# Attention with a running bound: rough tiles with a causal mask are computed inside exact tiles with a mask, the others in rounds without masks, four in every round

## The chip, the cores and the metric

The kernel runs on one core of one Trainium2 chip. Its engines are named as in the profile: PE is TensorE's matmul, PEld its weight load, DVE is VectorE, ACT is ScalarE, POOL is GpSimd, SP is SyncE, which here issues most of the DMAs. The metric is the time of one execution on the device, in microseconds (us). Three runs of the kernel before took 3304.9, 3312.74 and 3315.3 us; the median, 3312.74 us, is what the change is compared with.

## The reference, cut to what matters

A decoder of two layers over a sequence of 2048 tokens and 1024 channels: a gated DeltaNet layer, then a cross-decoder layer with "forgetting attention". Only the attention is touched. It has 16 heads of width 64; for query t and key s, with F the cumulated log forget gates:

```python
for blk in range(seq // B_BLOCK):
    ...
    logits = (jnp.einsum('bhqd,bhkd->bhqk', q[:, :, s0:s1], k[:, :, :s1]).astype(jnp.float32)
              + log_f_cum[:, :, s0:s1, None] - log_f_cum[:, :, None, :s1])
    causal = jnp.arange(s0, s1)[:, None] >= jnp.arange(s1)[None, :]
    p = jax.nn.softmax(jnp.where(causal, logits, -jnp.inf), axis=-1)
    outs.append(jnp.einsum('bhqk,bhkd->bhqd', p.astype(v.dtype), v[:, :, :s1]))
...
return (o * jax.nn.silu(z)) @ w_out
```

The softmax needs, for every query, something near the largest logit to subtract before the exponential.

## The kernel before

**The stages.** The program is five stages one after the other: projection and solve of the DeltaNet layer, its recurrence, an output projection, then `projections_and_attention` (the tiles whose names begin with `at_`), then a second output projection. Only `projections_and_attention` is changed. It first makes K, Q, V and the gate z of all heads by matmuls of a 128x128 weight with 512 columns, in 8 groups of 16 tiles of 24 matmuls each, and stores them to memory. Then comes the attention.

**Units and rounds.** A unit is a pair of heads p (0 to 7) and a block of 512 queries qb (0 to 3): 32 units, numbered u, for pair 0 with qb = 0, 1, 2, 3 and for every other pair with qb = 3, 2, 1, 0. Unit u covers 4(qb+1) key tiles of 128 keys; a round R handles two of these key tiles for both heads, so a unit has 2(qb+1) rounds and there are 160 rounds. From round 20 on the pattern repeats every 20 rounds (one pair of heads): 8, 6, 4 and 2 rounds.

**Exact tiles.** In a round PE makes four exact tiles of logits (keys on the partitions, queries along the free axis): a first pass over 67 rows (L1904) and a second over 128 rows (L1907), both in the format f32r and both up to 512 columns wide. In the last two rounds of a unit the key tiles cross the diagonal: the tiles are 512, 384, 256 or 128 columns wide, and a bf16 matmul of the identity with `mask_k` (L1906) adds the causal mask to 128 columns, between the two passes. ACT takes each tile through Exp (L2298); PE then multiplies the exponentials of the round before with V (L1922: eight matmuls for two key tiles), and DVE (head 0, L2146 and L2138) and POOL (head 1, L1685 and L1680) add up the exponentials for the denominator. At a unit's end, one round later, PE sums these over the partitions (L1936).

**Rough tiles.** The value that is subtracted is a row maximum of rough logits, found before the unit begins: for each head and each of four groups of 128 queries (`sub`), a one-pass matmul over 66 rows (L1890) against each block of 512 keys (`grp`), in a bank of PSUM out of three, which DVE reduces to its maximum (L2083). Where `grp == qb` the tile crosses the diagonal: it is (sub+1)*128 columns wide and gets the mask by a bf16 matmul with `mask_q` (L1893). I call these masked rough tiles and the others, always 512 wide, whole ones. There are 640 rough tiles: 384 whole and 256 masked. A rough tile on PE waits until DVE has reduced the one three places earlier (`reduced.wait(pe, j - 3)`).

**The order of the rough tiles** is a table made by Python code: `ITEMS` lists them unit by unit with `grp` innermost, and `ROUGHS[slot]` says which of them are done in which slot. The last 8 tiles of the projections (slots -8 to -1) are each followed by 6 rough tiles; after that the code spreads the rest over the rounds so that each unit is ready four rounds before it starts, which comes to 4 in most rounds, and 3 or 2 after round 132. In a round, each exact tile is followed by one rough tile. When the last rough tile of a unit is reduced, at the end of round `TURN[u]` PE transposes the maxima (L1944), ACT copies them (L2240) and issues two DMAs (L2243) that put them as a row into the tile of queries; the unit's first exact tile waits for them (`top_in`).

**The loads.** SP loads the keys, queries, gates and values of pair p+2 into the buffers of pair p, block by block of 512 positions: for each block `load_one` (the rows that the rough tiles need, L1704), `load_gates` (L1707), `load_two` (L1715), `load_values` (L1721), 2 MB in all. For p of 1 and more each block is loaded when the unit that used it last is done; for pair 0 all four blocks of pair 2 (first 3, then 2, 1, 0) are loaded one after the other when unit 3 is done, in round 21. The first rough tile of a unit waits for all blocks it needs.

## Time and profile before

| | |
|---|---|
| median of three runs (lowest, highest) | 3312.74 us (3304.9, 3315.3) |
| profiled execution: time, span | 3323.32 us, 3321.7 us |
| mean granted clock of TensorE in it | 0.962 of full speed |
| PE, DVE, ACT, POOL busy in the span | 3072.7, 1749.2, 1241.4, 1062.4 us |
| rough tiles: PE matmuls without masks (L1890), DVE reductions (L2083) | 238.0 us, 372.5 us (640 of each) |
| exact tiles: first pass, second pass, Exp on ACT | 263.3 us, 256.0 us, 332.1 us (640 of each) |

The profiled execution lasted 10.6 us longer than the median of the three others, within their spread on the high side. A duration of a PE matmul in the trace includes the way through the array: successive matmuls of 512 columns overlap, so what counts for the sum is the distance from one start to the next. The engine to look at is PE, and the stretch is the attention: from 2259.56 us (first rough tile) to about 3111 us of the span.

### The profile page before, as it was taken

How to read it: one execution, taken by the hardware profiler on the slowest of the kernel's cores; microseconds unless marked ns; L12 is line 12 of the kernel's file. 1: busy time of each engine (PE TensorE's matmuls, PEld its weight loads, DVE VectorE, ACT ScalarE, POOL GpSimd, SP SyncE). 2: the span in 40 equal slices, each digit the busy share in tenths (PEclk: the TensorE clock that was granted, in tenths of full speed). 3: DMA queues.
4: the chain of work that ended last, by engine and by line, in shares of the span. 5: the costliest groups of instructions: out<-in, count | busy, mean ns of one | idle time of the engine just before them, and what ended most of it. 6: DMA issues, size and time to landing. Idle time of an engine off the chain costs nothing. (4 is left out here: it accounts for less than half of the span.)

```text
span 3321.7 us, 40715 instructions
## 1 busy us (share of the span) xinstructions
PE 3072.7 (93%) x15148; PEld 2310.0 (70%) x15148; DVE 1749.2 (53%) x2715; ACT 1241.4 (37%) x2163; POOL 1062.4 (32%) x765
## 2 busy tenths in 40 slices
PE   5999899999987997995899999999999999999799
PEld 3766667888767886784687888887555555555487
DVE  4555564567464665554322221113777777777433
ACT  4245445554413554324322211210444444445411
POOL 0488970223216552110000000000355445555310
PEclk8999999999998999997899999998899999999899
DMA  5233431576736664556443431216353433330343
GB/s 217 65 132 109 136 107 52 180 231 185 236 99 211 209 201 151 184 179 186 114 114 107 125 102 70 76 60 143 90 128 96 115 85 88 87 90 10 108 152 120
DMA packets 259823, 427.86 MB, mean 129 GB/s; under 512 B 74126, under 2 KB 154646, under 8 KB 254508
## 3 DMA queue, kind: packets, MB, share of 16 engines
q1 hardware_dynamic: 220572, 323.54, 33.0%
q0 software_dynamic: 22960, 86.08, 8.3%
q10 hardware_dynamic: 16112, 15.86, 1.5%
q8 instruction: 111, 1.82, 0.2%
q14 instruction: 68, 0.56, 0.1%
HBM read 274.58 MB, written 150.69 MB: 128 GB/s over the span
## 5 line engine op out<-in xcount | busy, mean ns | idle before, releaser
L2298 ACT ACTIVATE at_probs<-at_ps 128x512 f32<-128x512 f32 (+3 forms) x640 | 332.1, 534 | 363.5 <-PE at_ps L1907 299.5
L2083 DVE TENSOR_REDUCE at_partial<-at_ps 128x1 f32<-128x512 f32 (+3 forms) x640 | 372.5, 606 | 161.1 <-PE at_ps L1890 121.7
L106 PE MATMUL pa_y<-pa_h_high,pa_w_high 128*128 128x512 f32 x1056 | 422.0, 400 | 12.8 <-ACT pa_acc L772 7.1
L108 PE MATMUL pa_y<-pa_h_high,pa_w_low 128*128 128x512 f32 x1056 | 412.7, 391 | 0.0
L107 PE MATMUL pa_y<-pa_h_low,pa_w_high 128*128 128x512 f32 x1056 | 412.5, 391 | 0.0
L1685 POOL TENSOR_TENSOR at_plain<-at_plain,at_probs 128x512 f32<-128x512 f32 (+3 forms) x256 | 308.2, 1204 | 230.1 <-ACT at_probs L2298 215.0
L1825 PE MATMUL at_ps<-at_h_high,at_w_high 128*128 128x512 f32 x768 | 301.2, 392 | 30.0 <-DVE at_w_low L2013 28.2
L1826 PE MATMUL at_ps<-at_h_low,at_w_high 128*128 128x512 f32 x768 | 300.2, 391 | 0.0
L1827 PE MATMUL at_ps<-at_h_high,at_w_low 128*128 128x512 f32 x768 | 300.1, 391 | 0.0
L1904 PE MATMUL at_ps<-at_h_low,at_h_high 67*128 67x512 f32 (+3 forms) x640 | 263.3, 411 | 10.8 <-ACT at_probs L2298 10.6
L1907 PE MATMUL at_ps<-at_h_low,at_h_high 128*128 128x512 f32 (+3 forms) x640 | 256.0, 400 | 0.0
L1890 PE MATMUL at_ps<-at_h_high,at_h_low 66*128 66x512 f32 (+3 forms) x640 | 238.0, 377 | 7.7 <-DVE at_partial L2083 6.6
L106 PEld LDWEIGHTS pa_y<-pa_h_high,pa_w_high 128*128 128x128 f32 x1056 | 199.3, 189 | 64.4 <-issue 15.7
L2146 DVE TENSOR_TENSOR at_plain<-at_plain,at_probs 128x512 f32<-128x512 f32 (+3 forms) x256 | 220.6, 862 | 19.1 <-ACT at_probs L2298 18.3
L107 PEld LDWEIGHTS pa_y<-pa_h_low,pa_w_high 128*128 128x128 f32 x1056 | 199.4, 189 | 43.8 <-issue 3.6
L108 PEld LDWEIGHTS pa_y<-pa_h_high,pa_w_low 128*128 128x128 f32 x1056 | 199.0, 188 | 42.3
L1904 PEld LDWEIGHTS at_ps<-at_h_low,at_h_high 67*128 67x128 f32 x640 | 124.3, 194 | 115.2 <-issue 81.8
L570 DVE SCALAR_TENSOR_TENSOR pa_acc<-pa_ybuf,pa_taps,pa_acc 128x2048 f32<-128x2048 f32 x72 | 196.7, 2733 | 2.6
L1825 PEld LDWEIGHTS at_ps<-at_h_high,at_w_high 128*128 128x128 f32 x768 | 145.2, 189 | 60.3 <-issue 28.6
L407 POOL TENSOR_SCALAR pa_gb<-pa_gb,pa_csil 128x1024 f32<-128x1024 f32 x48 | 169.6, 3534 | 30.3 <-DMA pa_gb<-in_a_mod_w_dram 20.7
L1827 PEld LDWEIGHTS at_ps<-at_h_high,at_w_low 128*128 128x128 f32 x768 | 145.0, 189 | 30.6
L1826 PEld LDWEIGHTS at_ps<-at_h_low,at_w_high 128*128 128x128 f32 x768 | 145.1, 189 | 30.0
(350 smaller groups left out, 5560.1 us busy)
## 6 DMA issues: line engine op xcount, KB each, us to landing
at_h_low<-s_Q SPq DMA_DIRECT2D x96, 256.0 KB, 7.1
s_qkv<-pa_sil POOLq DMA_DIRECT2D x16, 1024.0 KB, 6.6
pa_sil<-s_qkv SPq DMA_DIRECT2D x16, 1024.0 KB, 6.6
dr_kv<-s_qkv SPq DMA_DIRECT2D x16, 1024.0 KB, 8.7
s_K<-at_parts SPq DMA_DIRECT2D x64, 256.0 KB, 4.2
s_Q<-at_parts SPq DMA_DIRECT2D x64, 256.0 KB, 4.1
at_h_high<-s_K SPq DMA_DIRECT2D x32, 512.0 KB, 5.6
pa_wraw<-in_a_w_in_dram ACTq DMA_DIRECT2D x15, 1024.0 KB, 6.1
```

Source lines behind the costliest of these rows:

```text
L106: nc.tensor.matmul(out, w_high[:, k], h_high[:, k], start=k == 0, stop=False)
L107: nc.tensor.matmul(out, w_high[:, k], h_low[:, k], start=False, stop=False)
L108: ins = nc.tensor.matmul(out, w_low[:, k], h_high[:, k], start=False, stop=k == KC - 1)
L1685: g_summed.done(g_.tensor_tensor(to[:, off:BLK], to[:, off:BLK], xs[:, t, off:BLK], ALU.add))
L1825: mm(Y[b % NB], w_high[:, k, at], h_high[:, n, k], start=k == 0, stop=False)
L1826: mm(Y[b % NB], w_high[:, k, at], h_low[:, n, k], start=False, stop=False)
L1827: ins = mm(Y[b % NB], w_low[:, k, at], h_high[:, n, k], start=False, stop=k == KC - 1)
L1890: ins = mm(bank[:, 0:width], Q1[p % 2][0:DH + 2, h, q_at], K1[p % 2][0:DH + 2, h, grp * BLK:grp * BLK + width], start=True, stop=grp < qb)
L1904: mm(out, K1[s][0:DH + 3, h, k_at], Q1[s][0:DH + 3, h, q_at], start=True, stop=False)
L1907: logits_ok.done(mm(out, K2[s][:, h, k_at], Q2[s][:, h, q_at], start=False, stop=True))
L2083: reduced.done(v.tensor_reduce(partial[:, u % 2, h * NQ + sub, grp:grp + 1], rough[:, j % 3, 0:width], AX.X, ALU.max))
L2298: probs_ok.done(a.activation(probs[:, R % 2, t, h, off:BLK], logits[:, l % 3, off:BLK], ACT.Exp))
```

## The change

The list of rough tiles is no longer in the order of units. `whole(u)` gives the whole tiles of unit u, by falling `grp` and with heads and `sub` inside; `masked(u)` its eight masked ones. The eight slots behind the last projection tiles take 8 rough tiles each in place of 6: masked tiles of unit 0, whole and masked ones of unit 1, and the whole ones of units 2 and 3. In the rounds, the last two rounds of every unit (those whose exact tiles have a mask) take four masked rough tiles; the other rounds after round 6 take four whole ones; a round for which the list is empty takes none. That is so in rounds 2, 3, 6, 143 to 145, 148 to 151 and 154 to 159.

On PE the place of a rough tile inside its round changes too. In a round with masks, the rough matmul is issued between the exact tile's first pass and its mask, and the two mask matmuls stand one behind the other. In a round without masks nothing changes: a rough tile still follows each exact tile. A rough tile now waits for the two blocks it reads (`grp` and `qb`) instead of the unit's first one waiting for all. The partial maxima get room for eight units instead of two (`partial`).

Units are ready (`TURN`) in other rounds than before; rounds 48 to 67 stand for the repeating pattern:

| unit (pair, qb) | starts in round | maxima turned, before | after |
|---|---|---|---|
| 10 (2, 1) | 54 | 46 | 48 |
| 11 (2, 0) | 58 | 48 | 54 |
| 12 (3, 3) | 60 | 56 | 58 |
| 13 (3, 2) | 68 | 62 | 61 |

The diff, whole but for the context:

```diff
-    ITEMS = [(u, h, sub, grp) for u, (_, qb) in enumerate(UNITS) for h in range(2) for sub in range(NQ) for grp in range(qb + 1)]
-    ITEM_END = [2 * NQ * sum(qb + 1 for _, qb in UNITS[:u + 1]) for u in range(len(UNITS))]
+    def whole(u):
+        return [(u, h, sub, grp) for grp in reversed(range(UNITS[u][1])) for h in range(2) for sub in range(NQ)]
+
+    def masked(u):
+        return [(u, h, sub, UNITS[u][1]) for h in range(2) for sub in range(NQ)]
 
     EARLY = 8
-    PER_TILE = ITEM_END[2] // EARLY
+    ITEMS = masked(0) + whole(1) + masked(1) + whole(2) + whole(3)
+    PER_TILE = len(ITEMS) // EARLY
     ROUGHS = {s - EARLY: range(s * PER_TILE, (s + 1) * PER_TILE) for s in range(EARLY)}
-    DONE = ITEM_END[2]
+    wholes = [x for u in range(NB, len(UNITS)) for x in whole(u)]
+    maskeds = [x for u in range(2, len(UNITS)) for x in masked(u)]
     for R in range(ROUNDS):
-        due = [(ITEM_END[u] - DONE, max(START[u] - 4, 0)) for u in range(len(UNITS)) if ITEM_END[u] > DONE]
-        take = max([-(-n // (d - R + 1)) for n, d in due if d >= R], default=0)
-        ROUGHS[R] = range(DONE, DONE + take)
-        DONE += take
-    TURN = {u: 1 + next(s for s in ROUGHS if ITEM_END[u] - 1 in ROUGHS[s]) for u in range(len(UNITS))}
+        of = maskeds if R >= START[UNIT_OF[R] + 1] - 2 else wholes if R > START[2] else []
+        ROUGHS[R] = range(len(ITEMS), len(ITEMS) + min(4, len(of)))
+        ITEMS += of[:4]
+        del of[:4]
+    UNIT_END = [max(j for j, x in enumerate(ITEMS) if x[0] == u) for u in range(len(UNITS))]
+    UNIT_BEGIN = [min(j for j, x in enumerate(ITEMS) if x[0] == u) for u in range(len(UNITS))]
+    TURN = {u: 1 + next(s for s in ROUGHS if UNIT_END[u] in ROUGHS[s]) for u in range(len(UNITS))}
...
-                if j == 0 or ITEMS[j - 1][0] != u:
-                    for n in range(qb + 1):
+                if h == 0 and sub == 0:
+                    for n in (grp, qb):
                         pe.wait_ge(one_in[p % 2][n], (p // 2 + 1) * ONE)
...
-                if grp == qb:
-                    ins = mm(bank[:, sub * P:width], ident_b[:, :], mask_q[:, :], start=False, stop=True)
-                rough_ok.done(ins)
-
-            def exact_logits(R, t, kb, off, h):
+                if grp < qb:
+                    rough_ok.done(ins)
+
+            def mask_rough(j):
+                u, h, sub, grp = ITEMS[j]
+                if grp == UNITS[u][1]:
+                    rough_ok.done(mm(rough[:, j % 3, sub * P:(sub + 1) * P], ident_b[:, :], mask_q[:, :], start=False, stop=True))
+
+            def exact_logits(R, t, kb, off, h, beside):
...
                 if kb >= qb * NQ:
+                    for j in beside:
+                        rough_logits(j)
                     mm(logits[:, l % 3, off:off + P], ident_b[:, :], mask_k[:, :], start=False, stop=False)
+                    for j in beside:
+                        mask_rough(j)
                 logits_ok.done(mm(out, K2[s][:, h, k_at], Q2[s][:, h, q_at], start=False, stop=True))
+                if kb < qb * NQ:
+                    for j in beside:
+                        rough_logits(j)
...
-                            exact_logits(R, t, kb, off, h)
-                            for j in items[(2 * t + h) * part:(2 * t + h + 1) * part]:
-                                rough_logits(j)
+                            exact_logits(R, t, kb, off, h, items[2 * t + h:2 * t + h + 1])
```

Two places show what PE is given. The first is PE at the start of round 66, the first masked round of unit 12 (`at_h_low,at_h_high` is an exact pass, `at_h_high,at_h_low` a rough tile, `at_mask_k` and `at_mask_q` the masks). Before:

```order
L1904 MATMUL at_ps<-at_h_low,at_h_high 128x512
L1906 MATMUL at_ps<-at_mask_k,at_ident_b 128x128
L1907 MATMUL at_ps<-at_h_low,at_h_high 128x512
L1890 MATMUL at_ps<-at_h_high,at_h_low 128x128
L1893 MATMUL at_ps<-at_mask_q,at_ident_b 128x128
L1904 MATMUL at_ps<-at_h_low,at_h_high 128x512
L1906 MATMUL at_ps<-at_mask_k,at_ident_b 128x128
L1907 MATMUL at_ps<-at_h_low,at_h_high 128x512
```

The same place in the changed program, where L1915 and L1922 are the exact passes, L1897 the rough tile, L1919 and L1905 the masks:

```order
L1915 MATMUL at_ps<-at_h_low,at_h_high 128x512
L1897 MATMUL at_ps<-at_h_high,at_h_low 128x128
L1919 MATMUL at_ps<-at_mask_k,at_ident_b 128x128
L1905 MATMUL at_ps<-at_mask_q,at_ident_b 128x128
L1922 MATMUL at_ps<-at_h_low,at_h_high 128x512
L1915 MATMUL at_ps<-at_h_low,at_h_high 128x512
L1897 MATMUL at_ps<-at_h_high,at_h_low 128x256
L1919 MATMUL at_ps<-at_mask_k,at_ident_b 128x128
```

The rough matmul moved ahead of the exact tile's mask, and the two bf16 matmuls are neighbours. The second place is PE in slot -7, behind the second of the last eight projection tiles. Before, six rough tiles and the first matmul of the next projection tile:

```order
L1890 MATMUL at_ps<-at_h_high,at_h_low 128x384
L1893 MATMUL at_ps<-at_mask_q,at_ident_b 128x128
L1890 MATMUL at_ps<-at_h_high,at_h_low 128x512
L1893 MATMUL at_ps<-at_mask_q,at_ident_b 128x128
L1890 MATMUL at_ps<-at_h_high,at_h_low 128x512
L1890 MATMUL at_ps<-at_h_high,at_h_low 128x128
L1893 MATMUL at_ps<-at_mask_q,at_ident_b 128x128
L1890 MATMUL at_ps<-at_h_high,at_h_low 128x512
L1890 MATMUL at_ps<-at_h_high,at_h_low 128x256
L1893 MATMUL at_ps<-at_mask_q,at_ident_b 128x128
L1838 MATMUL at_ps<-at_w_high,at_h_high 128x512
```

In the changed program the same slot has eight whole rough tiles in a row (one row with its count), and then the first transpose of maxima and the next projection tile:

```order
L1846 MATMUL at_ps<-at_w_low,at_h_high 128x512
L1847 MATMUL at_ps<-at_w_high,at_h_low 128x512
L1897 MATMUL at_ps<-at_h_high,at_h_low 128x512 x8
L1962 MATMUL at_ps<-at_ident,at_top 8x128
L1845 MATMUL at_ps<-at_w_high,at_h_high 128x512
```

Six of the eight slots look like this one; slots -8 and -6 have eight masked rough tiles.

## Rows read from the trace of the kernel before

**Rows 1.** Stretches: us, busy PE, PEld, DVE, ACT, POOL (instructions), PEclk, DMA share, GB/s.

```profile
2259.56:2330.95 71.39, 64.94 (x243) 47.87 (x242) 28.39 (x56) 0.53 (x2) 6.96 (x2) 0.86 0.59 140
2330.95:2360.22 29.27, 29.27 (x91) 17.21 (x90) 17.50 (x28) 9.66 (x19) 7.71 (x8) 0.53 0.95 220
2360.22:2437.51 77.29, 76.64 (x374) 42.91 (x372) 65.25 (x98) 36.79 (x70) 40.37 (x33) 1.00 0.03 11
2437.51:2536.85 99.34, 96.79 (x486) 54.22 (x484) 75.69 (x125) 47.62 (x92) 48.98 (x41) 1.00 0.63 141
2536.85:3025.54 488.69, 480.68 (x2413) 270.09 (x2411) 375.21 (x618) 237.96 (x460) 250.26 (x206) 1.00 0.35 88
3025.54:3106.13 80.59, 79.73 (x390) 41.65 (x388) 58.77 (x78) 41.90 (x81) 46.50 (x37) 1.00 0.04 14
```

**Rows 2.** Waits in rounds 48 to 67: engine, line, releaser, us, times, longest.

```profile
PEld at_ps L1904 <- ACT at_probs L2298: 2.8, 4, 0.8
```

**Rows 3.** Timeline of a burst of six rough tiles, slot -5: start, us, instruction.

```profile
2288.06 0.69 DVE L2074 TENSOR_TENSOR at_parts<-at_ps,at_row 128x512 f32<-128x512 f32 x1 [6.35 <-PE at_ps L1840]
...
2288.67 3.27 DVE L2083 TENSOR_REDUCE at_partial<-at_ps 128x1 f32<-128x512 f32 x6
...
2290.71 0.57 PE L1838 MATMUL at_ps<-at_w_high,at_h_high 128*128 128x512 f32 x1
```

**Rows 4.** The same columns for rounds 51, 54, 55, 66 and 67.

```profile
2591.82:2596.76 4.94, 4.94 (x24) 2.78 (x22) 4.69 (x7) 2.40 (x4) 2.87 (x3) 1.00 0.06 22
...
2605.87:2609.70 3.83, 3.83 (x24) 2.78 (x22) 2.77 (x5) 2.39 (x4) 0.20 (x1) 1.00 0.00 0
2609.70:2615.49 5.79, 5.79 (x27) 3.06 (x25) 5.74 (x9) 3.62 (x6) 4.69 (x4) 1.00 0.52 133
...
2664.99:2670.27 5.28, 5.28 (x31) 2.70 (x30) 3.89 (x9) 2.18 (x4) 2.88 (x3) 1.00 0.00 0
2670.27:2675.17 4.90, 4.43 (x32) 2.68 (x30) 2.67 (x7) 1.37 (x5) 1.41 (x3) 1.00 0.02 4
```

**Rows 5.** Timeline of masks in rounds 66 and 67, PE.

```profile
2668.22 0.23 PE L1893 MATMUL at_ps<-at_mask_q,at_ident_b 128*128 128x128 bf16 x1
2668.38 0.65 PE L1922 MATMUL at_ps<-at_probs,at_parts 128*64 128x512 f32 x2
...
2670.48 0.23 PE L1906 MATMUL at_ps<-at_mask_k,at_ident_b 128*128 128x128 bf16 x1
...
2670.72 0.23 PE L1890 MATMUL at_ps<-at_h_high,at_h_low 66*128 66x128 f32 x1
```

**Rows 6.** Timeline: PE, fourth exact tile of round 67, behind the transpose for unit 14.

```profile
2672.72 0.33 PE L1904 MATMUL at_ps<-at_h_low,at_h_high 67*128 67x128 f32 x1 [0.47 <-ACT at_probs L2298]
```

**Rows 7.** Timeline, SP: last DMA issued for block 3 and for block 2 of pair 2.

```profile
2447.71 1.48 SPq L1721 DMA_DIRECT2D at_wraw<-s_ZT  x1
...
2453.34 0.51 SPq L1721 DMA_DIRECT2D at_wraw<-s_ZT  x1
```

**Rows 8.** The same loads: DMA issues from 2447.6 and from 2453.2 us, us to landing.

```profile
at_wraw<-s_ZT SPq DMA_DIRECT2D x1, 256.0 KB, 9.2
at_wraw<-s_ZT SPq DMA_DIRECT2D x1, 256.0 KB, 13.3
```

**Rows 9.** Timeline, PE: first rough tile of round 23, and of round 28.

```profile
2452.65 0.40 PE L1890 MATMUL at_ps<-at_h_high,at_h_low 66*128 66x512 f32 x1
2452.88 0.40 PE L1904 MATMUL at_ps<-at_h_low,at_h_high 67*128 67x512 f32 x1
...
2479.19 0.51 PE L1890 MATMUL at_ps<-at_h_high,at_h_low 66*128 66x512 f32 x1 [0.53 <-DMA at_h_high<-s_Fp]
```

**Rows 10.** The clock around an idle PE of the first stage, and in rounds 0 to 3.

```profile
347.40:352.10 4.70, 0.00 (x0) 0.00 (x0) 0.00 (x0) 4.64 (x3) 4.62 (x3) 1.00 0.44 121
352.20:355.50 3.30, 2.89 (x4) 1.34 (x5) 0.00 (x0) 3.28 (x6) 3.30 (x2) 0.50 0.95 308
...
2332.00:2359.20 27.20, 27.20 (x82) 16.40 (x82) 16.45 (x26) 9.57 (x19) 6.69 (x7) 0.50 0.98 229
```

More of the change, by code:

```diff
@@ L1537, in projections_and_attention @@
         mask_q, mask_k = st.sb("mask_q", [P, P], BF16), st.sb("mask_k", [P, P], BF16)
-        partial = st.sb("partial", [P, 2, 2 * NQ, NB])
+        partial = st.sb("partial", [P, 2 * NB, 2 * NQ, NB])
         top = st.sb("top", [P, 2, 2 * NQ])
@@ L1960, in _ @@
                                 rough_logits(j)
+                                mask_rough(j)
                             for u in turned_in(slot):
@@ L1979, in _ @@
                         pe.wait_ge(top_in, 32 * (u + 1))
-                    part = -(-len(items) // 4)
                     for t, kb, off in tiles(R):
                         for h in range(2):
-                            exact_logits(R, t, kb, off, h)
-                            for j in items[(2 * t + h) * part:(2 * t + h + 1) * part]:
-                                rough_logits(j)
+                            exact_logits(R, t, kb, off, h, items[2 * t + h:2 * t + h + 1])
                 for summed in ended(R, 1):
@@ L2079, in reduce @@
                 width = BLK if grp < qb else (sub + 1) * P
-                if j == 0 or ITEMS[j - 1][0] != u:
-                    top_ok.wait(dve, u - 2)
+                if j == UNIT_BEGIN[u]:
+                    top_ok.wait(dve, u - 2 * NB)
                 rough_ok.wait(dve, j)
-                reduced.done(v.tensor_reduce(partial[:, u % 2, h * NQ + sub, grp:grp + 1], rough[:, j % 3, 0:width], AX.X, ALU.max))
-                if j == ITEM_END[u] - 1:
+                reduced.done(v.tensor_reduce(partial[:, u % (2 * NB), h * NQ + sub, grp:grp + 1], rough[:, j % 3, 0:width], AX.X, ALU.max))
+                if j == UNIT_END[u]:
                     reduced.wait(dve, j)
                     turned_ok.wait(dve, u - 2)
-                    top_ok.done(v.tensor_reduce(top[:, u % 2], partial[:, u % 2, :, 0:qb + 1], AX.X, ALU.max))
+                    top_ok.done(v.tensor_reduce(top[:, u % 2], partial[:, u % (2 * NB), :, 0:qb + 1], AX.X, ALU.max))
             make_columns(0)
```

## The prediction

> **What bounds the kernel now.** I read the stretches of the attention first [rows 1]. In all of them PE is busy for 91 to 100% of the time, DVE for 40 to 84%, ACT and POOL for less: PE bounds the attention. Beside the first two stretches the granted clock is 1.00. The waits come next: in rounds 48 to 67, 98 us long, PE's largest wait for another engine is 2.8 us in four times [rows 2]. So a change pays here only if it shortens PE's own sequence, and costs wherever PE is made to stand still. Then I read the one place where PE already waits for DVE, the bursts of rough tiles between projection tiles [rows 3], single rounds [rows 4], single masks [rows 5], what follows the transpose of the maxima [rows 6], the loads that rough tiles wait for [rows 7 to 9], and the clock after an idle PE [rows 10]. All sums are for the profiled execution (3323.32 us, its span 3321.7); the median of the three runs is 3312.74, 10.6 us lower, and I add the difference to that.
>
> **The bursts, +8.8 us.** PE runs at most three rough tiles ahead of DVE. In a burst DVE first takes the projection tile (its start is 0.26 us into the burst), then starts its reductions 0.61 us later, and six of them took 3.27 us, which is 0.6 us from one 512-column start to the next (the narrow ones less) [rows 3]. The burst of six ended 2.92 us after its start of 2287.79 (at 2290.71). With eight whole tiles the last one waits for the fifth reduction: 0.88 us to the first, four more starts of 0.6, 0.73 from a start until PE goes on, and 0.23 for the tile itself: 4.24 us. With eight masked tiles the fifth reduction starts at 0.88 + 1.6 = 2.5 us, and the burst is 3.1 us long. So 6 x 4.24 + 2 x 3.1 = 31.6 us. Before, the eight bursts took 2.3 to 3.2 us each in the timeline, 22.8 us of the stretch of 71.39 us; the other 48.6 us are seven projection tiles at a clock of 0.86 on the mean [rows 1]. I take these as unchanged: the clock falls after the bursts already now, and can hardly fall more often than once in each.
>
> **Rounds 0 to 3, -4.3 us.** They took 29.27 us at a mean clock of 0.53 [rows 1]. Sixteen rough tiles become eight narrow ones; in rounds 2 and 3 eight tiles go without anything in their place. At half clock a 512-column pass is 0.43 us: eight are 3.4 us, and the narrower tiles of rounds 0 and 1 make 0.9.
>
> **The rounds with and without masks.** A full round with four whole rough tiles: round 51 took 4.94 us with one masked tile of full width [rows 4], and a mask before the values costs 0.16 us from L1893 to L1922 [rows 5], against 0.10 where the values follow a f32r pass: 4.87. A unit's first round, whose values are those of narrow tiles: 3.83 less the mask, more 128 columns, 3.82. With the sums of the unit before: 5.79 - 0.07 = 5.72. Round 66, four masked rough tiles already, becomes 5.28 - 0.25 = 5.03; round 67, 4.90 with a stall of 0.66 [rows 6], becomes 4.11; unit 11's two rounds, with the same reckoning, 3.95 and 4.97.
>
> The stalls behind `turn_top`: ACT copies the maxima and issues two DMAs ahead of its next Exp, and an exact tile of the next round waits for it, with an engine idle for 0.47 us in round 67 [rows 6] (0.66 more than usual from start to start) and 0.45 in a full round. After the change three of four fall in full rounds, one in a short one that is at that tile 0.1 us sooner: 3 x 0.45 + 0.76 = 2.1 us.
>
> Twenty rounds are then 6 x 4.87 + 3 x 5.72 + 3 x 3.82 + 3 x 5.03 + 3.95 + 3 x 4.11 + 4.97 + 2.1 = 96.3 us, against 98.2 in the trace, -1.9. Rounds 40 to 139: 5 x 96.3 = 481.5 against 488.69, -7.2 (the last seven rounds had three rough tiles before). Rounds 4 to 19 in the same way: 75.7 against 77.29, -1.6. Rounds 140 to 157, where eleven rounds lose their rough tiles and four take masked pairs: 77.6 against 80.59, -3.0; POOL's and DVE's work there (46.5 and 58.8 us [rows 1]) stays covered.
>
> The Trainium skill ("TensorE: Matmul & The Clock Gate", Architectural detail) says that PE pulls weight loads ahead of matmuls in flight. By that a lone mask would cost its columns alone and the pairing nothing: the sum would come out some 8 us later. The 0.24 us above speak against it.
>
> **A new wait, +6.4 us less 0.9.** Rough tiles of unit 8 move from round 28 to round 23, and the first needs block 2 of pair 2. In the trace these blocks arrive in order under a saturated DMA: the last DMA of block 3 was issued at 2447.71 [rows 7] and landed 9.2 us later [rows 8], at 2456.9; that of block 2, issued at 2453.34, landed at 2466.6. What the rough tile waits for is the first quarter of block 2's bytes: 2456.9 + 9.7/4 = 2459.3. The cross-check is round 28, where the first rough tile waited for block 0 until 2479.19 [rows 9], two blocks or 20 us later. PE would be at that rough tile at 2452.65 [rows 9], plus 0.25 for rounds 21 and 22 as changed: 2452.9. It stands there 6.4 us, and behind it in PE's queue are three exact tiles of round 23, for which ACT, DVE and POOL wait. The 0.9 us of round 28 go. Nothing else can hide this, since all work of PE is in that queue. Block 1, needed in round 25, comes in time. Rounds 20 to 39: 96.3 + 6.4 = 102.7 against 99.34, +3.4 (the 0.9 is in the 99.34).
>
> **The clock behind it, +6 us.** An idle PE of 4.7 us in the first stage was followed by a clock of 0.50 [rows 10], the 1.2 GHz level, there for 3.4 us, until the clock was at 1.00 again while dense f32r passes of 128 rows ran. In the attention it took longer: from 2332.0 to 2359.2 the clock stayed at 0.50 with PE busy in all 27.2 us [rows 10], and rose inside the values of round 3, behind the sums of unit 0. So after the stall of round 23 I expect half clock. The bounds: 3.4 us of it, which costs 1.7; or until the sums in round 29, six rounds of about 4.2 us each, 25 us. Neither is nearer by its kind of work than the second, but the values at half clock last twice as long as now and may end it earlier; I take one and a half rounds, 6 us.
>
> The Trainium skill (same page, What's actually happening) has the gate open again after one busy window. By it the 6 would be 1.7. Rows 10 disagree for this stage, and the measurement decides.
>
> **Sum.** 8.8 - 4.3 - 1.6 + 3.4 - 7.2 - 3.0 + 6 = +2.1 us. 3312.74 + 2.1 = 3314.8; I say 3315.
>
> **Rivals.** (1) Slower by the clock: after round 23 it stays at 1.2 GHz until the sums of round 29, or does not come back in round 3: 3312.7 - 3.9 + 25 = 3334, and in between from 3323 on, when it lasts three rounds or more. For it: the 27.2 us [rows 10]. Against: the rise came with the values, and those run in each round. (2) DVE becomes the bound in rounds of four whole tiles. In round 51 it was busy for 4.69 of 4.94 us [rows 4]; a fourth whole tile in place of narrower ones adds up to 0.4 us in the others. If it lags 0.2 us in each of some 60 such rounds, +12: 3327. Against: DVE's lag may grow by three tiles, the two masked rounds of each unit give it time, and round 51 already is such a round and did not stall. (3) The second mask costs 0.13: 232 pairs x 0.07 = 16 us more, 3331; this is also the case that the pairing doesn't do what it says. (4) Faster: block 2 arrives in time, because its first DMAs pass the queue sooner than by their share of bytes. Then 6.4 and 6 go: 3302.5. For it: rough tiles wait for rows of only two blocks. Against: the order of landings above.
>
> **How the numbers follow.** My forecast 0.52; (1) 0.18, (2) 0.05, (3) 0.08, (4) 0.12, the skill's rule on weight loads 0.05 (3323). A run can be told from no change at about 0.3%, 10 us: under 3302.8 or over 3322.7. Slower: (1), (3), half of (2) and of the rule, 0.31. Faster: 0.10 of (4) and 0.06 for the forecast with a clock that rises at once and bursts cheaper than worked out, 0.16. The rest, 0.53, is no difference. Range: 3301 to 3331; my forecast alone 3306 to 3322.
>
> **What would show it.** Bursts of 4.2 us between projection tiles; in masked rounds 0.18 us for both masks; rounds 51 and 66 at 4.87 and 5.03; 96.3 us for rounds 48 to 67; a wait of some 6 us of PE in round 23 for a DMA into `at_h_high`, and a PEclk of 0.5 behind it. A stretch of 98 us for rounds 48 to 67 would refute the pairing, no wait in round 23 the fifth term, and a clock of 1.00 behind that wait the sixth.

## The result: 0.43% slower, and the profile after

The changed kernel took 3328.07 us (median of 6 runs, 3322.8 to 3331.8), the kernel before 3314.02 us beside it (6 runs, 3304.9 to 3332.5): a ratio of 1.0043 with a 95% interval of 1.0023 to 1.0064. The 14 us more lie in the predicted range (3301 to 3331), but above the 3306 to 3322 of the forecast alone, and on the side that had a chance of 0.31, not on the likeliest one, "no difference".

The profiled execution of the changed kernel took 3328.63 us. Its stretches, in the columns of [rows 1]: us, busy PE, PEld, DVE, ACT, POOL, PEclk, DMA share, GB/s:

```profile
2264.57:2342.02 77.45, 69.88 (x252) 48.33 (x250) 39.98 (x73) 0.53 (x2) 6.96 (x2) 0.90 0.55 134
2342.02:2363.58 21.56, 20.54 (x87) 12.19 (x85) 9.67 (x19) 9.12 (x19) 6.68 (x7) 0.72 1.06 236
2363.58:2439.78 76.20, 75.47 (x377) 42.14 (x375) 57.94 (x94) 36.41 (x70) 40.11 (x34) 1.00 0.07 25
2439.78:2547.21 107.43, 98.97 (x486) 55.70 (x485) 79.41 (x125) 47.45 (x92) 46.70 (x41) 0.95 0.59 133
2547.21:3031.55 484.34, 476.17 (x2423) 270.85 (x2421) 393.96 (x625) 237.25 (x460) 241.16 (x206) 1.00 0.35 89
3031.55:3111.11 79.56, 77.03 (x374) 39.65 (x372) 43.83 (x67) 40.00 (x81) 45.33 (x37) 1.00 0.04 14
```

Line by line against [rows 1]: the last projection tiles with their bursts +6.1, rounds 0 to 3 -7.7, rounds 4 to 19 -1.1, rounds 20 to 39 +8.1, rounds 40 to 139 -4.4, rounds 140 to 157 -1.0. The sum is nothing, and the remaining 5.3 us between the two profiles had arisen ahead of 2259 us, in stages that are the same in both. A single pair of profiles therefore does not show the 14 us; this is what the experiments had to settle first.

A burst of eight whole rough tiles, slot -4 (it answers to [rows 3]); timeline: start, us, instruction:

```profile
2303.66 0.86 PE L1897 MATMUL at_ps<-at_h_high,at_h_low 66*128 66x512 f32 x3
...
2304.53 4.87 DVE L2099 TENSOR_REDUCE at_partial<-at_ps 128x1 f32<-128x512 f32 x8
2305.26 2.89 PE L1897 MATMUL at_ps<-at_h_high,at_h_low 66*128 66x512 f32 x5 [0.74 <-DVE at_partial L2099]
2307.99 0.40 PE L1845 MATMUL at_ps<-at_w_high,at_h_high 128*128 128x512 f32 x1
```

Three tiles start at once, then PE waits for DVE, tile by tile. The burst lasts 4.33 us, from 2303.66 to 2307.99.

Rounds 51, 54, 55, 59, 66 and 67 of the changed kernel (it answers to [rows 4]), same columns as above:

```profile
2601.22:2606.10 4.88, 4.88 (x23) 2.69 (x21) 4.71 (x7) 2.39 (x4) 2.81 (x3) 1.00 0.25 90
2615.16:2619.00 3.84, 3.84 (x23) 2.71 (x22) 2.80 (x5) 2.39 (x4) 0.21 (x1) 1.00 0.00 0
2619.00:2625.29 6.29, 5.99 (x28) 2.87 (x26) 6.29 (x8) 3.56 (x7) 4.05 (x4) 1.00 0.41 101
2638.33:2644.09 5.76, 5.09 (x35) 2.85 (x33) 3.42 (x8) 2.60 (x7) 2.43 (x4) 1.00 0.56 142
2675.14:2680.17 5.03, 5.03 (x34) 2.95 (x33) 2.94 (x6) 2.42 (x5) 2.44 (x2) 1.00 0.01 3
2680.17:2684.21 4.04, 4.04 (x24) 2.36 (x24) 2.40 (x7) 1.32 (x5) 1.18 (x2) 1.00 0.00 0
```

Rounds 51, 54, 66 and 67 are where the prediction put them (4.87, 3.82, 5.03, 4.11). Rounds 55 and 59 were put at 5.72 and 4.97 us, with a wait behind the maxima of 0.45 and 0.76 on top: 6.17 and 5.73, against 6.29 and 5.76. In round 55 DVE is busy for all of the 6.29 us, and PE is idle for 0.30.

The masks of round 66 (it answers to [rows 5]), timeline of PE:

```profile
2675.07 0.28 PE L1897 MATMUL at_ps<-at_h_high,at_h_low 66*128 66x256 f32 x1
2675.19 0.23 PE L1919 MATMUL at_ps<-at_mask_k,at_ident_b 128*128 128x128 bf16 x1
2675.26 0.22 PE L1905 MATMUL at_ps<-at_mask_q,at_ident_b 128*128 128x128 bf16 x1
2675.29 0.48 PE L1922 MATMUL at_ps<-at_h_low,at_h_high 128*128 128x512 f32 x1
2675.61 0.34 PE L1915 MATMUL at_ps<-at_h_low,at_h_high 67*128 67x384 f32 x1
```

From start to start the two masks take 0.07 and 0.03 us, and the f32r pass behind them 0.32 instead of 0.23: 0.19 us for the pair, against 0.18 worked out.

Round 23, the new wait of PE (timeline), and the clock behind it (the columns of [rows 10]):

```profile
2462.62 0.80 PE L1897 MATMUL at_ps<-at_h_high,at_h_low 66*128 66x512 f32 x1 [6.74 <-DMA at_h_high<-s_Fp]
```

```profile
2455.90:2462.62 6.72, 0.00 (x0) 0.00 (x0) 0.00 (x0) 0.60 (x1) 0.09 (x1) 0.80 1.08 209
2462.62:2470.16 7.54, 7.54 (x18) 3.91 (x18) 5.31 (x6) 1.79 (x3) 2.54 (x2) 0.50 1.10 212
```

The wait is 6.74 us (6.4 predicted), and 7.54 us of busy PE follow at a clock of 0.50, the lower of the two levels, which costs half of them, 3.8 us (6 predicted).

### The profile page after: what moved, and what is told of

It reads as the page before. It is cut to its first block and busy times, and to the rows that moved or that the text cites. A ratio compares the mean times of both kernels' runs of the same rounds, so it can differ in the third digit from the quotient of the medians.

```text
span 3327.0 us, 40755 instructions
## 1 busy us (share of the span) xinstructions
PE 3068.6 (92%) x15148; PEld 2306.8 (69%) x15148; DVE 1753.6 (53%) x2715; ACT 1237.6 (37%) x2163; POOL 1045.8 (31%) x765
## 5 line engine op out<-in xcount | busy, mean ns | idle before, releaser
L1692 POOL TENSOR_TENSOR at_plain<-at_plain,at_probs 128x512 f32<-128x512 f32 (+3 forms) x256 | 301.3, 1177 | 251.8 <-ACT at_probs L2314 237.9
L1915 PE MATMUL at_ps<-at_h_low,at_h_high 67*128 67x512 f32 (+3 forms) x640 | 255.0, 398 | 13.8 <-ACT at_probs L2314 13.6
L1922 PE MATMUL at_ps<-at_h_low,at_h_high 128*128 128x512 f32 (+3 forms) x640 | 255.2, 399 | 0.0
L1897 PE MATMUL at_ps<-at_h_high,at_h_low 66*128 66x512 f32 (+3 forms) x640 | 239.8, 380 | 14.7 <-DMA at_h_high<-s_Fp 6.7
L108 PEld LDWEIGHTS pa_y<-pa_h_high,pa_w_low 128*128 128x128 f32 x1056 | 199.3, 189 | 42.2
L1915 PEld LDWEIGHTS at_ps<-at_h_low,at_h_high 67*128 67x128 f32 x640 | 122.9, 192 | 131.4 <-issue 92.1
```

The source lines that it names most:

```text
L108: ins = nc.tensor.matmul(out, w_low[:, k], h_high[:, k], start=False, stop=k == KC - 1)
L1692: g_summed.done(g_.tensor_tensor(to[:, off:BLK], to[:, off:BLK], xs[:, t, off:BLK], ALU.add))
L1897: ins = mm(bank[:, 0:width], Q1[p % 2][0:DH + 2, h, q_at], K1[p % 2][0:DH + 2, h, grp * BLK:grp * BLK + width], start=True, stop=grp < qb)
L1915: mm(out, K1[s][0:DH + 3, h, k_at], Q1[s][0:DH + 3, h, q_at], start=True, stop=False)
L1922: logits_ok.done(mm(out, K2[s][:, h, k_at], Q2[s][:, h, q_at], start=False, stop=True))
```

## The experiments

**The same two kernels again.** Both were run again, for the spread of their stages.

> The changed kernel unchanged, for the spread of its stages from one execution to the next. Theory A (the difference is made in the attention stage): with 3 further profiled executions of either kernel in hand, the attention stage from its first rough tile to the end costs the changed kernel within 1 us of 849.4, and the time stands some 0 to 4 us above the kernel before. Theory B (the stages before the attention differ by themselves): the start of the first rough tile, 2264.9 us in the profile after and 2259.6 in the profile before, moves by 3 us or more between executions of the same kernel, and the 14 us between the medians are mostly made there or by the clock, so that the ratio here may come out anywhere from 0.999 to 1.006.

> The kernel before the change, unchanged, for a second profiled execution of it: the one shown took 3323.3 us, 9 us above the median of 23 runs (3314.4). Theory A (the profile of before was an unfavourable one, by TensorE's clock ahead of round 4: it stood at half from 2331.9 to 2359.2 us, and rounds 0 to 3 took 29.27 us where all profiles of the changed list show 21.5 to 22.5): here rounds 0 to 3 take 21 to 25 us, or the projection tiles less than 48.5 us, the time is near 3314, and the stretch from the start of the program to round 4 takes 2349 to 2354 us and not 2360.2; rounds 4 to 159 stay within 1 us of 749.0. Theory B (the 9 us are lost in the stages ahead of the attention or in its rounds): the first rough tile starts at 2255 or earlier, with rounds 0 to 3 at 29 us again.

> The same kernel once more, for a third profiled execution. Theory A: as for the second. If the second and the third differ by more than 5 us at the start of round 4, the clock ahead of it is a draw from execution to execution, and single profiles can't be compared there.

The changed kernel took 3329.69 us (ratio 1.0047, 1.0029 to 1.0065), the kernel before 3310.22 us (10 runs, ratio 0.9996, 0.9977 to 1.0015) and, in its third profile, 3332.45 us. Of the two theories on the changed kernel neither holds: the attention took 2.9 us more than in its first profile and the time stayed 15 us above the kernel before, which A had at 0 to 4; and though the start of the attention moves, by 2 us between the two profiles of the changed kernel and by 6 among the three of the kernel before, the 14 us are not made there, as B had it. The profiled stretches of all five in us (bursts and projection tiles told apart by the starts of their first matmuls):

| | before | before, 2nd | before, 3rd | changed | changed, 2nd |
|---|---|---|---|---|---|
| bursts, slots -8 to -1 | 22.9 | 22.8 | 23.0 | 33.6 | 34.1 |
| projection tiles between them | 48.5 | 42.2 | 48.4 | 43.9 | 49.1 |
| rounds 0 to 3 | 29.3 | 17.9 | 29.3 | 21.6 | 21.5 |
| start of the program to round 4 | 2360.2 | 2346.4 | 2366.3 | 2363.6 | 2367.1 |
| rounds 20 to 39 | 99.3 | 102.0 | 102.2 | 107.4 | 104.7 |
| rounds 40 to 139 | 488.7 | 488.7 | 488.7 | 484.3 | 484.3 |

In the second profile of before, the first two stretches and the one of rounds 20 to 39 read:

```profile
2263.59:2328.56 64.97, 58.52 (x243) 43.27 (x242) 28.39 (x56) 0.53 (x2) 6.96 (x2) 0.95 0.65 154
2328.56:2346.41 17.85, 17.30 (x92) 10.38 (x91) 15.67 (x28) 9.45 (x19) 7.14 (x8) 1.00 1.00 241
...
2423.63:2525.63 102.00, 98.29 (x486) 55.10 (x485) 75.86 (x125) 47.61 (x92) 49.02 (x41) 0.98 0.63 138
```

The kernel before has two outcomes ahead of round 4: rounds 0 to 3 at a clock of 1.00 in 17.9 us, or at 0.53 in 29.3 us. The profile that the prediction was made from had the second. Theory A on the kernel before holds in direction: the second profile gained more than it said (round 4 at 2346.4 us, not 2349 to 2354), and its rounds behind round 4 took 2.6 us more, not within 1, because of a wait in round 28. The third profile repeats the bad outcome. Yet the bad outcome seems to be the rare one: of the 97 executions of the kernel before that the experiments brought, 11 have a mean clock of 0.959 to 0.962, as those two profiles have (0.962 and 0.961), and these 11 took 3322.9 to 3332.6 us; the ones near the median stand at 0.964 to 0.966, the second profile at 0.965. What decides between the outcomes no run shows.

All six profiles with the long bursts gave 20.9 to 22.5 us for rounds 0 to 3, and the start of round 4 at 2363.6 to 2369.1 us. Taking the time behind round 4 off the medians (961.5 to 964.5 us before, 960.6 to 963.5 changed, and 1.6 us around the span), round 4 begins at about 2349 us in a median run of before and at about 2364 us in one of the changed kernel. The loss is made ahead of round 4; behind it the new wait (2.5 to 8 us more in rounds 20 to 39) uses up what the list gains (1.1, 4.4 and 1.0 us).

**Block 2's rows first.** SP's loads for pair 2, in another order:

```diff
-                for n in fetch:
-                    gated.wait(sp, u)
-                    for part in (load_one, load_gates, load_two, load_values):
-                        part(sp, p + 2, n)
+                fetch = list(fetch)
+                if fetch:
+                    gated.wait(sp, u)
+                for parts_now in ((load_one, load_gates), (load_two, load_values)):
+                    for n in fetch:
+                        for part in parts_now:
+                            part(sp, p + 2, n)
```

> The fetches of the third pair of blocks are issued by SP in another order: the row blocks and gates of all four slots first, then the two value blocks of each. All else is the changed kernel's. Theory A (round 23 waits because the row block of slot 2 lands behind the value blocks of slots 0 and 1, and the half clock behind it comes from that wait): the 6.74 us wait of TensorE is gone or under 1 us, the clock does not fall to 0.50 in round 23 (10.2 us there, worth about 3.9 us), rounds 20 to 39 take 97 to 98 us and not 107.4, and the kernel is 9 to 11 us faster than the changed one. Rival (the clock falls there anyway, or the wait only moves to the value blocks): 0 to 7 us faster. Rival (the time of the changed kernel was lost outside the attention): the same 10 us faster than the changed kernel, which still leaves it 2 to 6 us above the kernel before; by theory A it ends 6 to 10 us below it.

3320.53 us, 9.2 below the changed kernel's 3329.69; ratio to before 1.0020 (1.0009 to 1.0031). Rounds 20 to 39:

```profile
2439.88:2536.79 96.91, 95.19 (x487) 54.17 (x485) 78.80 (x125) 47.51 (x92) 47.05 (x41) 1.00 0.62 148
```

The wait and the half clock are gone, and 10.5 us with them (7.8 against the changed kernel's second profile, whose wait was 4.71 us). Theory A is right on the mechanism; that it leaves 6 us above the kernel before is what the rival said.

**Masks apart.** In masked rounds the rough tile and its mask went back behind the exact tile's second pass, where they stood before the change:

```diff
-                    for j in beside:
-                        rough_logits(j)
                     mm(logits[:, l % 3, off:off + P], ident_b[:, :], mask_k[:, :], start=False, stop=False)
-                    for j in beside:
-                        mask_rough(j)
                 logits_ok.done(mm(out, K2[s][:, h, k_at], Q2[s][:, h, q_at], start=False, stop=True))
-                if kb < qb * NQ:
-                    for j in beside:
-                        rough_logits(j)
+                for j in beside:
+                    rough_logits(j)
+                    mask_rough(j)
```

(The text on record puts the old place of the rough tile ahead of the third pass; as the diff shows, it is behind it.)

> The changed list of rough tiles, but in the rounds with a mask the rough tile and its mask stand where they stood before the change: the rough tile between the exact logits and the third pass, its mask behind it, so that the two masks of a round no longer stand side by side. Theory A (a mask that follows a mask costs 0.06 us, and one that stands alone 0.12 and another 0.12 of the instruction behind it): masked rounds take 5.26 and 4.24 us in place of 5.02 and 4.04, about 0.2 us each in some 60 masked rounds, 13 us in all. Rival (the order of the masks costs nothing that TensorE does not pay anyway): masked rounds within 0.05 us of the changed kernel, 0 to 3 us in all.

3342.97 us (1.0083, 1.0064 to 1.0103), 13.3 more than the changed kernel. Rounds 66 and 67 took 5.25 and 4.23 us. Start of round 66:

```profile
2681.59 0.23 PE L1917 MATMUL at_ps<-at_mask_k,at_ident_b 128*128 128x128 bf16 x1
2681.63 0.48 PE L1918 MATMUL at_ps<-at_h_low,at_h_high 128*128 128x512 f32 x1
2681.95 0.22 PE L1897 MATMUL at_ps<-at_h_high,at_h_low 66*128 66x128 f32 x1
2682.01 0.23 PE L1905 MATMUL at_ps<-at_mask_q,at_ident_b 128*128 128x128 bf16 x1
2682.05 0.48 PE L1915 MATMUL at_ps<-at_h_low,at_h_high 67*128 67x512 f32 x1
2682.37 0.23 PE L1917 MATMUL at_ps<-at_mask_k,at_ident_b 128*128 128x128 bf16 x1
```

Each mask takes only 0.04 us to the next start, but the 512-column f32r pass behind it takes 0.32, not 0.23. Two masks apart pay that twice. Theory A is confirmed, to the size. The Trainium skill ("TensorE: Matmul & The Clock Gate", Architectural detail) says that weight loads are pulled ahead of matmuls in flight. The prediction drew from it that the order would cost nothing; for a bf16 matmul between f32r ones the 0.32 us and the 13.3 us speak against that conclusion.

**Six tiles in a burst.** As before the change. The sixteen tiles left over, two from each burst, go into rounds 2, 3, 6 and 7, and the whole tiles behind them stand one such round later (the text on record counts eight):

```diff
-    ITEMS = masked(0) + whole(1) + masked(1) + whole(2) + whole(3)
+    ITEMS = masked(0) + whole(1) + masked(1) + whole(2) + whole(3)[:8]
...
-    wholes = [x for u in range(NB, len(UNITS)) for x in whole(u)]
+    wholes = whole(3)[8:] + [x for u in range(NB, len(UNITS)) for x in whole(u)]
...
-        of = maskeds if R >= START[UNIT_OF[R] + 1] - 2 else wholes if R > START[2] else []
+        of = maskeds if R >= START[UNIT_OF[R] + 1] - 2 else wholes if R >= START[1] else []
```

> Six rough tiles in each burst of the first eight steps, as before the change, and not eight to ten; the eight left over of the fourth unit go into rounds 2, 3, 6 and 7, and the fetch of the third pair starts as before, so that the wait for its third block stands one round later. Theory A: the bursts fall from 33.4 to 23 to 25 us (-8.4 to -10.4), rounds 2, 3, 6 and 7 gain 8 tiles at 0.5 us (+4), the wait of round 23 (6.74 us) shrinks by the 4.9 us of one round and with it the half clock behind it (-3.9): 5 to 13 us faster than the changed kernel. Rival (TensorE's clock decides: more bursts kept the clock up between the projection tiles, 43.9 us against 48.5, and rounds 0 to 3 at 21.6 against 29.3 us): the shorter bursts bring back the half clock in the projection tiles and in rounds 0 to 3, +4.6 and +7.7, and the kernel is 1 us faster to 7 us slower than the changed one.

3312.45 us, 17.2 below the changed kernel and the same as before (0.9999, 0.9988 to 1.0009). The bursts took 24.0 us, the projection tiles 40.3, rounds 0 to 3 21.9, rounds 20 to 39 97.2 with no wait left. Theory A in direction, but both predicted too little: round 4 starts at 2354.8 us, 9 to 12 us sooner than in the two profiles of the changed kernel, and with unit 8's tiles in round 24 and not 23 no wait was left in this profile. The wait alone is worth 9.2 us by the experiment on the loads, which leaves 8 of the 17.2 for the bursts.

**The gate later, the transfers of the maxima later, and both.** Rounds 40 to 139 gave 4.4 us and not 7.2. In round 61 the fourth rough tile waits for DVE; in round 55 an exact tile seems to wait for ACT, and ACT for DVE (timeline of round 55):

```profile
2619.64 1.19 ACTq L2259 DMA_DIRECT2D at_h_low<-at_minus_top  x2
2620.54 0.68 DVE L2170 TENSOR_TENSOR at_plain<-at_ps,at_wraw 128x512 f32<-128x512 f32 x1
2621.01 1.08 ACT L2314 ACTIVATE at_probs<-at_ps 128x512 f32<-128x512 f32 x2 [1.40 <-DVE at_plain L2154]
...
2621.66 0.50 PE L1915 MATMUL at_ps<-at_h_low,at_h_high 67*128 67x512 f32 x1 [0.30 <-ACT at_probs L2314]
```

Three kernels were made. In one DVE does the first two reductions of a round ahead of `gate(u)`; in one ACT copies the maxima as before but issues their two transfers behind the second Exp of the next round; the third has both, with the six-tile bursts as well. A further one had six tiles and the gate. The gate:

```diff
+                items = ROUGHS[R] if R < ROUNDS else []
+                half = 2 * -(-len(items) // 4)
+                for j in items[:half]:
+                    reduce(j)
                 for u in ended(R, 1):
                     gate(u)
                 if R < ROUNDS:
-                    items, first = ROUGHS[R], R == START[UNIT_OF[R]]
-                    half = 2 * -(-len(items) // 4)
-                    for j in items[:half]:
-                        reduce(j)
+                    first = R == START[UNIT_OF[R]]
```

The transfers, cut at "...":

```diff
+                if TURN[u] < 0:
+                    send_top(u)
+
+            def send_top(u):
+                p, qb = UNITS[u]
                 minus_ok.wait(act, u)
...
                             probs_ok.done(a.activation(probs[:, R % 2, t, h, off:BLK], logits[:, l % 3, off:BLK], ACT.Exp))
+                        if t == 0 and R:
+                            for u in turned_in(R - 1):
+                                send_top(u)
```

> The changed kernel, but in a unit's first round VectorE does the two first reductions of rough logits before it multiplies the finished outputs by their gates, not behind it. Theory A (in the first round of a unit the fourth rough tile waits for its bank because the gate, 0.68 us, stands ahead of the reductions): the wait of 0.49 us ahead of it is gone, full first rounds take 5.75 to 5.85 us in place of 6.28 and 6.08, 0.35 us each in 24 of them, and all is 6 to 9 us faster than the changed kernel. Rival (VectorE is at its bound there, and the wait moves to the values of the new unit, whose bank the gate frees, or to the next round): 0 to 2 us faster, or slower.

> Both edits together: six rough tiles in each of the first bursts, and the gate behind the first two reductions. By theory A their gains add up, since they stand in different rounds: 3304 to 3307 us, 0.2 to 0.3% below the kernel before. Rival (the gate's place gains nothing): 3312, as with six tiles alone.

> The changed kernel, but ScalarE issues the two transfers of a unit's maxima not ahead of the four Exp of the next round, only behind the second of them; the copy of the maxima stays where it is. Theory A (the fourth exact tile of the next round waits for an Exp that stands behind these two issues, 0.58 and 0.61 us, and this is what the prediction's 2.1 us for 20 rounds is): that tile starts at 2.2 us of its round in place of 2.65 to 2.7, the waits of TensorE for the Exp (8.4 us in 21 waits between 2470 and 2990 us) are gone, rounds 40 to 139 take 474 to 477 us and not 484.3, and the whole is 10 to 14 us faster than the changed kernel. Rival (ScalarE or VectorE has no room there, and the wait comes back one tile or one round later, or the maxima land too late for the unit that starts two rounds after): 0 to 4 us faster, with a wait of the first exact tile of a unit for the transfer.

> Three edits together: six rough tiles in each of the first bursts, the gate behind the first two reductions, and the transfers of the maxima behind the second Exp of the next round. If the gains add up: 3311 less 10 to 14, 3297 to 3301 us, 0.4 to 0.5% below the kernel before. If the last one gains nothing: 3309 to 3312 us, as without it.

| kernel | median us | ratio to before (95%) | rounds 40 to 139 |
|---|---|---|---|
| changed | 3328 to 3330 | 1.0047 (1.0029 to 1.0065) | 484.3 |
| gate later | 3327.72 | 1.0040 (1.0026 to 1.0053) | 483.2 |
| six tiles, gate later | 3311.17 | 0.9987 (0.9973 to 1.0000) | 482.8 |
| transfers later | 3316.95 | 1.0010 (0.9996 to 1.0024) | 478.8 |
| six tiles, gate and transfers later | 3288.51 | 0.9922 (0.9901 to 0.9942) | 469.8 |

Moving the gate gained 1.2 us in rounds 40 to 139 and at most 2 in all, as the rival had it (theory A wanted 6 to 9): round 61 went from 6.09 to 5.76, but round 55 stayed at 6.29, held by the Exp. With six tiles, too, the gate's place gained 1 us, where theory A had 5 to 8. Moving the transfers gained 11 to 13 us in all, as theory A said, but only 5.5 there, not 7 to 10: round 55 went to 6.02, and now the fourth rough tile waited in it for DVE:

```profile
2615.99 1.20 ACTq L2264 DMA_DIRECT2D at_h_low<-at_minus_top  x2
...
2617.39 0.19 PEld L1897 LDWEIGHTS at_ps<-at_h_high,at_h_low 66*128 66x128 f32 x1 [0.48 <-DVE at_partial L2099]
```

The [1.40 <-DVE] of the Exp is gone in this kernel though DVE's add L2154 stands as before: the Exp had waited for the two issues.

Both edits gained 14.5 us (the six-tile bursts leave this stretch at 484.4), 7.8 more than their sum of 6.7. There are two reasons, and round by round they make about 3 and 5 us. In rounds 49 and 55 one wait had covered the other: 6.29 us as changed, 6.29 with the gate alone, 6.02 with the transfers alone, 5.71 with both. And the transfers alone brought a new wait, which their rival had named: the first exact tile of a unit waited up to 1.4 us for the maxima, 5.3 us in five times. The gate starts SP's next loads, and there these were issued just ahead of the maxima (SP and ACT, then PE's wait, transfers alone):

```profile
2634.56 0.58 SPq L1711 DMA_DIRECT2D at_h_high<-s_K  x1
2634.91 1.22 ACTq L2264 DMA_DIRECT2D at_h_low<-at_minus_top  x2
...
2639.66 0.47 PE L1915 MATMUL at_ps<-at_h_low,at_h_high 67*128 67x512 f32 x1 [1.11 <-DMA at_h_low<-at_minus_top]
```

With the gate later too, the maxima go first (2613.50 us against 2614.36), and no such wait is left. That the loads ahead of them held them up is read from this order; no run tests it by itself. The whole kernel is 22.7 us faster than with six tiles and the gate, where adding up would have given 10 to 14. The same stretch and rounds 55 and 59 of that kernel:

```profile
2523.11:2992.91 469.80, 469.80 (x2423) 271.84 (x2421) 382.84 (x625) 241.03 (x460) 240.94 (x206) 1.00 0.35 92
```

```profile
2593.43:2599.14 5.71, 5.71 (x28) 2.96 (x26) 5.71 (x8) 3.77 (x7) 3.90 (x4) 1.00 0.11 40
...
2612.18:2617.07 4.89, 4.89 (x36) 2.78 (x34) 3.54 (x8) 2.71 (x7) 2.43 (x4) 1.00 0.25 64
```

PE is never idle in 469.8 us. DVE is still busy for all of round 55, and PE no longer waits.

**What the list is worth without those waits.** The kernel before with its own list and both edits, and the kernel with three edits with the loads of the other order:

> The kernel before the change with its own list of rough tiles, and with two of the three edits of the last kernel: the transfers of the maxima behind the second Exp of the next round, and the gate behind the first two reductions. It asks what the list itself is worth once no round waits for ScalarE or VectorE. Theory A (the list saves what the prediction said, mostly the second 0.06 us of every mask, but part of it was eaten by the waits in full rounds): rounds 40 to 139, 488.7 us with the waits, take 478 to 482 us here, against 469.8 with the changed list and the same edits, so the list is worth 8 to 12 us there and not the 4.4 measured between the two original kernels; the whole is 3302 to 3308 us. Rival (the edits do all the work, and the list is worth 4 us at most): rounds 40 to 139 take 470 to 475 us, and the whole about 3296 to 3300.

> The kernel with the three edits, and with the fetches of the third pair in the order of row blocks first. In the kernel with three edits TensorE again waited 3.17 us in round 24 and fell to the half clock for 3.4 us. Theory A: that wait goes here, rounds 20 to 39 take 94 us and not 99.0, and the whole is 3283 to 3285 us. Rival (the wait moves to the value blocks, or to the fetch of the row block behind them): 3287 to 3289 us.

The first took 3297.50 us (0.9953, 0.9935 to 0.9970). Its rounds 40 to 139:

```profile
2519.92:2994.27 474.35, 474.35 (x2413) 269.90 (x2411) 382.32 (x618) 241.39 (x460) 249.22 (x206) 1.00 0.36 92
```

474.35 against 469.80: the list is worth 4.55 us there without waits, and 4.35 with them. The rival holds, the waits did not eat the list's gain. In whole executions the list with six-tile bursts is worth 0.3% (0.9922 against 0.9953). The second took 3287.88 us (0.9933, 0.9912 to 0.9953): rounds 20 to 39 fell from 99.0 to 94.0 us in the profile, as theory A said, but the time is the same as that of the kernel with three edits, as the rival said. That kernel's row in round 24 was

```profile
2447.30 0.51 PE L1897 MATMUL at_ps<-at_h_high,at_h_low 66*128 66x512 f32 x1 [3.17 <-DMA at_h_high<-s_Fp]
```

So 5 us that one profile shows are lost in the spread of some 10 us between runs. These two kernels, with the changed list and the three edits, beat the kernel before by 0.7 to 0.8%.

## Why the prediction was right in its range and wrong in its sum

The sum said +2 and 14 were measured. That 3328 lies in the range is luck of a kind: the range reached so far up for a clock that stays at half behind round 23, for DVE falling behind in some 60 rounds and for a second mask at its full price, and none of the three came in that size. The new wait, its clock and the masks were right; what failed is the term of rounds 0 to 3.

**Bursts: right, a little small.** +8.8 predicted, +10.7 measured (22.9 to 33.6); bursts of whole tiles took 4.3 to 4.6, of masked ones 3.3 to 3.5 us.

**Rounds 0 to 3, -4.3: the step that failed.** "They took 29.27 us at a mean clock of 0.53", and everything was taken off that. 29.3 us was one of two outcomes; with the long bursts the stretch took 20.9 to 22.5 us in all six profiles, in the first 7.7 less than the one and 3.7 more than the other. In the median run of before it was the other, as its time and mean clock say; no profile of a median run shows it. With +3.7 in place of -4.3 the same sum gives +10, and with the bursts as measured +12, against 14 measured. The prediction warned itself (this profile was 10.6 us above the median) and only subtracted the difference, instead of asking in which stretch it lay. Why the long bursts give neither outcome stays open.

**Projection tiles, "unchanged": part of the same two outcomes.** Before, they took 48.5 and 48.4 us where rounds 0 to 3 took 29.3, and 42.2 where these took 17.9; with the long bursts 43.9 to 49.1 in six profiles. The clock decides, and it varies from run to run. Against the good outcome that is 2 to 7 us more, which no term holds.

**Rounds 4 to 19 and the single rounds: right.** -1.6 predicted, -1.1 measured.

**The new wait and the clock behind it: right.** 6.4 predicted, 6.74 and 4.71 measured, and 5.2 to 7.8 in the three other profiles with long bursts and the old order of loads; the clock's part was 3.8 in place of 6. Removing the cause gave back 9.2 us of time. What was missed is that before waits too: in its second profile 1.70 us in round 28, with half clock behind it, so the stretch rises by 2.5 to 8 us and not by 9.4.

```profile
2466.52 0.50 PE L1890 MATMUL at_ps<-at_h_high,at_h_low 66*128 66x512 f32 x1 [1.70 <-DMA at_h_high<-s_Fp]
```

The Trainium skill (same page, What's actually happening) has the gate open again after one busy window, which the prediction put at 1.7 us. Behind the 6.74 us the trace disagrees, with 3.8; behind the waits of 1.70 and 3.17 us the half clock lasted 3.4 us and cost those 1.7.

**Rounds 40 to 139, -7.2: mis-sized in the waits.** Without waits the rounds were worked out at 5 x 94.2 = 471.0 us and measured at 469.8. The waits were put at 5 x 2.1 = 10.5 and are 484.34 - 469.80 = 14.5. Behind the maxima they are 0.55 to 0.58 us in rounds 49, 55 and 62 (0.45 predicted) and 0.88 in round 59 (0.76): the pass that had to wait takes 0.33 us to the next start and not 0.23 (2621.66 to 2621.99 in round 55), which the prediction left out; and the 0.36 us of round 61, whose fourth rough tile stands behind DVE's gate (rival 2, in small), were not in the sum. The kernel before had as much, 488.73 - 474.35 = 14.4.

**Rounds 140 to 157, -3.0: measured -1.0.** The prediction named no wait behind the maxima here. Rounds 149 and 155 took 6.08 and 6.05 us without a rough tile, against 5.33 and 4.92 before with some, because the Exp stood behind the two issues in them; with the transfers moved each took 4.87, and rounds 140 to 157 took 76.6 us, 3.0 less than 79.6.

**Pairing of masks: right**, 0.19 us for a pair, and 13.3 us for the whole by experiment (the list makes 240 pairs in the rounds, not the 232 of the third rival).

## What to carry to other kernels

When the profiled run lies well off the median, find the stretch that makes the difference before taking terms from it; one more profile of the unchanged kernel with the other outcome, or the mean clocks of its other runs, could have turned this sum from +2 to +12. Two waits of one round can cover each other, and an edit that removes one wait can bring another: that an edit gains little alone says nothing on what two gain together (1.2 and 5.5 us apart, 14.5 together). And ask of every instruction ahead of a bottleneck's partner, here two transfer issues of 0.6 us on ScalarE, whether it could stand where that engine idles anyway.

## What the runs showed of the hardware

- The same program can go through the same stretch at two clocks: rounds 0 to 3 of the kernel before at 1.00 (17.9 us) or at 0.53 (29.3 us), with PE busy for 97 to 100% in both.
- A bf16 matmul of 128 columns between f32r matmuls costs 0.04 us itself and 0.09 in the next f32r pass; two in a row cost 0.07 and 0.03 themselves and the 0.09 once, 0.19 in place of 0.26.
- After a wait of 6.7 us the clock stayed at 0.50 for 7.5 us of busy PE. After shorter waits of 3.67 us (kernel before with two edits, round 28), 3.17 us (kernel with three edits, round 24) and 1.70 us (kernel before, second profile) it also fell, for 6.8, 3.4 and 3.4 us. Busy PE in the first two of these, columns as above:

```profile
2461.00:2467.80 6.80, 6.80 (x22) 4.86 (x23) 2.96 (x5) 2.06 (x4) 1.51 (x1) 0.50 0.66 151
...
2449.20:2452.60 3.40, 3.40 (x10) 1.15 (x10) 3.40 (x5) 1.02 (x2) 2.34 (x2) 0.50 1.15 221
```

- Two transfer issues filled 1.19 us of ScalarE's queue ahead of its next Exp (2619.64 to 2621.01 in round 55), though the profile puts that wait down to VectorE; with the issues moved it was gone.
